# Second feed-forward matmul by Strassen's seven products over pairs of blocks, operands through rings of four slots

## The reference, cut to what matters

```python
x = x + concatenate([y_lru, y_att], axis=-1) @ w_out[i]
h = rmsnorm(x, g_ffn[i])
x = x + square(relu(h @ w_ff1[i])) @ w_ff2[i]
gate = sigmoid(rmsnorm(x, g_ple[i]) @ w_ple_gate[i])
x = x + gate * (p[i] @ w_ple_proj[i])
return rmsnorm(x, g_final)
```

## Time and profile before

| | us |
|---|---|
| median of 3 runs | 1074.56 |
| lowest and highest | 1074.12, 1074.68 |
| span of the profiled execution, first to last instruction | 1072.1 |
| PE busy in it | 1063.0 |
| DVE, ACT, POOL busy | 680.3, 468.1, 416.6 |

### The profile page before, as it was taken

How to read it: one execution, slowest core, us unless ns; L and a number is a source line. 1 busy time by engine, 2 the same in 40 slices (tenths; PEclk the granted TensorE clock), 3 DMA queues, 4 the chain that set the end, 5 groups by cost and what they waited for, 6 DMA issues and landing times.

```text
span 1072.1 us, 13889 instructions
## 1 busy us (share of the span) xinstructions
PE 1063.0 (99%) x4960; PEld 869.5 (81%) x4960; DVE 680.3 (63%) x932; ACT 468.1 (44%) x806; POOL 416.6 (39%) x282
## 2 busy tenths in 40 slices
PE   9999999999999999999999999999999999999997
PEld 7877787777887888888888888888888888888897
DVE  7988787888799643644544544544544544697648
ACT  7467836555683332332332322322322422566334
POOL 0000061334136626516426425435435445295221
PEclk9999999999999999999999999999999999999999
DMA  8111110111011121121111111112112112420004
GB/s 335 40 40 40 40 58 32 40 41 40 0 40 40 40 79 39 39 78 39 39 70 48 39 49 69 39 39 78 39 39 78 39 39 76 159 79 1 1 2 158
DMA packets 20179, 61.06 MB, mean 57 GB/s; under 512 B 2096, under 2 KB 4144, under 8 KB 20144
## 3 DMA queue, kind: packets, MB, share of 16 engines
q1 hardware_dynamic: 19312, 59.56, 15.3%
q10 hardware_dynamic: 832, 1.05, 0.3%
HBM read 56.40 MB, written 4.19 MB: 57 GB/s over the span
## 4 chain that ended last, share of the span: by engine, by line
PE 89%; DVE 6%; ACT 3%; issue 1%; DMA 1%; SPq 0%; POOL 0%; DVEq 0%; ACTq 0%; POOLq 0%
PE bank L611 29%; PE bank L612 28%; PE bank L613 28%; PE bank L726 1%; PE bank L697 1%; ACT raw L1191 1%; DMA stage<-in_w_in 1%; DVE xT L1849 1%; DVE t_lo L1798 1%; PE bank L741 0%; PE bank L756 0%; DVE raw L1792 0%; ACT h_hi L1183 0%; DVE r_ffn L1433 0%; DVE r_mix L1433 0%
## 5 line engine op out<-in xcount | busy, mean ns | idle before, releaser
L611 PE MATMUL bank<-h_hi,w_hi 128*128 128x512 f32 (+1 forms) x722 | 278.5, 386 | 0.6 <-DVE w_lo L1428 0.5
L612 PE MATMUL bank<-h_lo,w_hi 128*128 128x512 f32 (+1 forms) x722 | 274.6, 380 | 0.0
L613 PE MATMUL bank<-h_hi,w_lo 128*128 128x512 f32 (+1 forms) x722 | 274.5, 380 | 0.0
L1849 DVE TENSOR_TENSOR xT<-bank,xT 128x512 f32<-128x512 f32 x256 | 172.3, 688 | 109.8 <-PE bank L613 109.8
L611 PE MATMUL bank<-u_hi,w_hi 128*128 128x512 f32 x512 | 199.8, 390 | 0.2
L613 PE MATMUL bank<-u_hi,w_lo 128*128 128x512 f32 x512 | 199.2, 389 | 0.0
L612 PE MATMUL bank<-u_lo,w_hi 128*128 128x512 f32 x512 | 199.2, 389 | 0.0
L611 PEld LDWEIGHTS bank<-h_hi,w_hi 128*128 128x128 f32 x722 | 135.7, 188 | 35.1 <-issue 6.6
L613 PEld LDWEIGHTS bank<-h_hi,w_lo 128*128 128x128 f32 x722 | 135.8, 188 | 26.1
L612 PEld LDWEIGHTS bank<-h_lo,w_hi 128*128 128x128 f32 x722 | 135.8, 188 | 25.4 <-issue 0.5
L557 POOL TENSOR_TENSOR w_lo<-w_raw,w_hi 128x1024 fp32r<-128x1024 f32 x30 | 73.9, 2485 | 125.6 <-ACT w_hi L1283 117.8
(11 more groups left out here) (238 smaller groups left out, 1727.9 us busy)
## 6 DMA issues: line engine op xcount, KB each, us to landing
w_raw<-in_w_ff SPq DMA_DIRECT2D x60, 512.0 KB, 3.8
stage<-in_w_in SPq DMA_DIRECT2D x13, 512.0 KB, 6.6
stage<-in_w_out SPq DMA_DIRECT2D x8, 512.0 KB, 4.5
stage<-in_w_ple_gate SPq DMA_DIRECT2D x8, 512.0 KB, 3.2
xT<-in_x SPq DMA_DIRECT2D x6, 512.0 KB, 10.9
stage<-in_w_ff SPq DMA_DIRECT2D x4, 512.0 KB, 3.2
out_x<-xT SPq DMA_DIRECT2D x4, 512.0 KB, 3.1
out_x<-xT SPq DMA_DIRECT2D x6, 256.0 KB, 2.2
```

What stands on the lines that cost most here:

```text
L611: pe.matmul(o, whi, hh, start=first, stop=False, skip_group_check=onto)
L612: pe.matmul(o, whi, hl, start=False, stop=False, skip_group_check=onto)
L613: return pe.matmul(o, wlo, hh, start=False, stop=last, skip_group_check=onto)
L1849: dve.tensor_tensor(dst, bank[4 + q % 4][:, :], dst, ALU.add).then_inc(y_added, 1)
```

## The change

Blocks 0 and 1 stay as they were. Blocks 2 to 15 are taken in seven pairs g = 1 to 7. A pair is 28 steps of 12 matmuls. Steps 0 to 13 are the seven first-matmul products of each of its two blocks (s = 0, 1), as before. Steps 14 to 27 are seven Strassen products of the second matmul: product p = 0 to 6 is summed over the pair's two blocks (s = 0, then s = 1), 4 tiles of output each. Products 1, 3 and 5 are added onto the banks of the product before, and DVE reads each of the seven sums into four tiles of xT (`read_sums`). The four quarters of x are not kept as such but in another basis of sums, put in place in front of the first pair (8 operations) and taken out again in the last (`fold`, 8 operations).

The left operand of each step (a weight quarter or a sum of quarters) goes through a ring of four slots: ACT copies the high part (`left_head`) once the step four before is over (`step_over`), POOL subtracts the low part (`left_low`). The right operands of steps 14 to 27 go through a second ring of four (`right_head` on ACT, `right_low` on DVE), and their sums are made by DVE (`right_sum`). POOL makes the weight sums: four for each first block (`w1_front`, `w1_back`) and eight for the pair's second weights (`w2_sum`). The first weights now come in halves, those of the second block of a pair behind `left_low` 3 and 6. The order of the k tiles in `gate` and `ple_high` is changed (FF_ORDER: 4 to 7, then 0 to 3), `pw_lo` moves from DVE to POOL, and the gate's second piece is loaded when steps 26 and 27 are over.

```diff
+PAIRS = FF_BLOCKS // 2
+STEPS = 4 * PRODUCTS
+LEFTS = 4
+RIGHTS = 4
...
+        def step_over(eng, g, t):
...
+            before, t = (1, t + STEPS) if t < 0 else (0, t)
+            if t < 2 * PRODUCTS:
+                eng.wait_ge(prod_done, 2 * PRODUCTS * g + (t - 6 - 2 * PRODUCTS * before))
+            elif t % 2 == 0:
+                eng.wait_ge(sub_done, PRODUCTS * g + ((t - 2 * PRODUCTS) // 2 - 6 - PRODUCTS * before))
+            else:
+                eng.wait_ge(ff2_done, STEPS * g + (4 * ((t - 2 * PRODUCTS) // 2) + 8 - STEPS * before))
...
-            with sp.Fori(2, FF_BLOCKS) as b:
-                sp.wait_ge(prod_done, PRODUCTS * b - PRODUCTS)
-                load_w1(b)
-                load_w2(b)
...
+            with sp.Fori(2, PAIRS) as g:
+                sp.wait_ge(left_ready, counted(10 - STEPS, g))
+                load_w1_half(g, 0, 0)
+                sp.wait_ge(left_ready, counted(17 - STEPS, g))
+                load_w1_half(g, 0, 1)
+                sp.wait_ge(left_ready, counted(27 - STEPS, g))
+                load_w2_pair(g)
+                sp.wait_ge(left_ready, counted(3, g))
+                load_w1_half(g, 1, 0)
+                sp.wait_ge(left_ready, counted(6, g))
+                load_w1_half(g, 1, 1)
...
+            def left_low(g, t):
+                pool.wait_ge(left_high, counted(t, g))
+                pool.tensor_tensor(left_lo[t % LEFTS], left_raw(t), left_hi[t % LEFTS], ALU.subtract
+                                   ).then_inc(left_ready, 1)
...
+            def w1_front(g, s):
...
+                for h in range(2):
+                    pool.wait_ge(w1_half_in[h], 32 * g + 16 * (s - 1))
+                pool.tensor_tensor(a21, a21, a22, ALU.add).then_inc(sum1_made, 1)
+                pool.wait_ge(sum1_made, counted(4 * s, g, 8))
...
+                pool.tensor_tensor(s2_raw(s), a21, a11, ALU.subtract).then_inc(sum1_made, 1)
...
+                pool.wait_ge(sum1_made, counted(4 * s + 1, g, 8))
+                pool.wait_ge(left_ready, counted(PRODUCTS * s + 2, g))
+                pool.tensor_tensor(a21, a22, s2_raw(s), ALU.subtract).then_inc(sum1_made, 1)
+                pool.wait_ge(sum1_made, counted(4 * s + 2, g, 8))
+                pool.tensor_tensor(s2_raw(s), a12, s2_raw(s), ALU.subtract).then_inc(sum1_made, 1)
...
+                    pool.wait_ge(left_ready, counted(2 * PRODUCTS - 1, g))
+                    pool.wait_ge(sum2_made, counted(2 + s, g, 8))
+                    ins = pool.tensor_tensor(s4_raw(s), a21, a12, ALU.subtract)
...
+            def left_pair(g):
+                for s in range(2):
+                    w1_front(g, s)
+                    for i in range(3):
+                        left_low(g, PRODUCTS * s + i)
+                    w1_back(g, s)
+                    for i in range(3, PRODUCTS):
+                        left_low(g, PRODUCTS * s + i)
+                        if s == 1 and i in (3, 4):
+                            w2_sum(g, 0, i - 3)
+                for s in range(2):
+                    left_low(g, 14 + s)
+                    w2_sum(g, 1, s)
+                for s in range(2):
+                    w2_sum(g, 2, s)
+                for t in range(16, 20):
+                    left_low(g, t)
+                for s in range(2):
+                    left_low(g, 20 + s)
+                    w2_sum(g, 3, s)
+                for t in range(22, STEPS):
+                    left_low(g, t)
...
+                pool.wait_ge(pw_high, h + 1)
+                pool.tensor_tensor(pw_lo[:, o], pw_raw[:, o], pw_hi[:, o], ALU.subtract).then_inc(pw_ready, 1)
+            pool.wait_ge(right_ready, counted(2 * PRODUCTS - 1, PAIRS - 1, 2 * PRODUCTS))
...
-            with pe.Fori(2, FF_BLOCKS) as b:
-                for i in range(PRODUCTS):
...
-                    product(b, i)
-                pe.wait_ge(w2_split, 2 * b)
-                ff2(b)
...
+            def second_product(g, p):
+                onto = p in (1, 3, 5)
+                for s in range(2):
+                    t, j = 2 * PRODUCTS + 2 * p + s, 2 * p + s
+                    pe.wait_ge(left_ready, counted(t, g))
+                    pe.wait_ge(right_ready, counted(j, g, 2 * PRODUCTS))
...
+                    for m in range(LT):
+                        if s == 0:
+                            pe.wait_ge(y_added, read_count(g, p - 1, m))
...
+                        if s == 1:
+                            last.then_inc(ff2_done, 1)
+                    if s == 0:
+                        last.then_inc(sub_done, 1)
+            with pe.Fori(1, PAIRS) as g:
+                for t in range(2 * PRODUCTS):
+                    first_product(g, t)
+                for p in range(PRODUCTS):
+                    second_product(g, p)
...
+            def left_head(g, t):
+                step_over(act, g, t - LEFTS)
+                left_raw_in(act, g, t)
+                act.activation(left_hi[t % LEFTS], left_raw(t), ACT.Copy).then_inc(left_high, 1)
+            def right_head(g, j):
+                if j >= RIGHTS:
+                    step_over(act, g, 2 * PRODUCTS + j - RIGHTS)
+                right_raw_in(act, g, j)
+                act.activation(right_hi[:, j % RIGHTS, :], right_raw(j), ACT.Copy).then_inc(right_high, 1)
...
+            def ff_pair(g, last=False):
+                for t in range(LEFTS):
+                    left_head(g, t)
+                for s in range(2):
+                    t = PRODUCTS * s + LEFTS
+                    first_bank(g, s)
+                    for i in range(4):
+                        left_head(g, t + i)
+                        if s == 1 and i == 0:
+                            right_head(g, 0)
+                    hidden_square(g, s, 0)
+                    left_head(g, t + 4)
+                    hidden_square(g, s, 1)
+                    last_bank(g, s)
+                    if s == 1:
+                        right_head(g, 1)
+                        right_head(g, 2)
+                    left_head(g, t + 5)
+                    hidden_square(g, s, 2)
+                    left_head(g, t + 6)
+                    hidden_square(g, s, 3)
+                right_head(g, 3)
+                for j in range(4, 2 * PRODUCTS):
+                    right_head(g, j)
+                    left_head(g, 14 + j)
+                    if last and j < 10:
+                        embedding_high(j - 4)
...
+            def post(g, s):
...
+                product_over(dve, g, PRODUCTS * s + 1)
...
+                dve.tensor_tensor(u2[:, :], bank[1][:, :], u2[:, :], ALU.add).then_inc(u2_made, 1)
+                product_over(dve, g, PRODUCTS * s + 2)
...
+                dve.tensor_tensor(c22, bank[3][:, :], u2[:, :], ALU.add).then_inc(p5_read, 1)
+                product_over(dve, g, PRODUCTS * s + 3)
...
+                dve.tensor_tensor(c22, bank[2][:, :], c22, ALU.add).then_inc(c22_made, 1)
...
+                relu_scale(c22, 0)
+                product_over(dve, g, PRODUCTS * s + 4)
+                dve.tensor_tensor(c12, bank[3][:, :], u2[:, :], ALU.add).then_inc(c12_made, 1)
...
+                relu_scale(c12, 0)
+                if s == 1:
+                    right_sum(g, 0, 1)
...
+                relu_scale(c11, 1)
+                if s == 1:
+                    right_low(g, 1)
+                    right_low(g, 2)
+                product_over(dve, g, PRODUCTS * s + 6)
+                dve.tensor_tensor(c21, bank[2][:, :], u2[:, :], ALU.add).then_inc(c21_made, 1)
...
+                relu_scale(c21, 1)
...
+            def read_sums(g, p):
+                for m in range(LT):
+                    dve.wait_ge(ff2_done, STEPS * g + (4 * p + m + 5))
...
+                    ins.then_inc(y_added, 1)
...
+            def fold(hf, m):
...
+                    ins = dve.tensor_tensor(dst, c22, dst, ALU.add)
...
+                ins.then_inc(folded, 1)
...
+            def hidden_pair(g, last=False):
+                post(g, 0)
+                right_sum(g, 0, 0)
+                right_low(g, 0)
+                post(g, 1)
+                right_low(g, 3)
+                right_sum(g, 1, 0)
+                right_sum(g, 1, 1)
+                for p in range(PRODUCTS):
+                    read_sums(g, p)
+                    if last and p == 4:
+                        for m in range(LT):
+                            fold(0, m)
+                    if last and p == 5:
+                        for m in range(LT):
+                            fold(1, m)
+                            ple_low(m, 0)
+                    if p < 5:
+                        right_low(g, 2 * p + 4)
+                        right_low(g, 2 * p + 5)
+                    if p in (0, 1):
+                        right_sum(g, 2 + p, 0)
+                        right_sum(g, 2 + p, 1)
+                    if last and p in (2, 3):
+                        embedding_low(2 * p - 4)
+                        embedding_low(2 * p - 3)
...
```

(42 more changed lines are left out.)

269 lines of the change are left out of this document (208 added, 61 removed).

## The result

The changed kernel takes 1125.74 us (median of 4 runs, 1123.36 to 1126.25) against 1074.59 us: 1.0475 times as long, with an interval of 1.046 to 1.0489. The forecast was 1084 and its range ended at 1100: the sign was right, the size was not. The profiled execution took 1125.94 us, its span is 1124.1 us.

A forecast was written before the change was run, and what follows sets the result against it. PE, busy 99%, was taken to bound the kernel. From 1072.1 us, less 38.1 saved, plus 7 × 5.1 of stall and 11.5 behind the loop, came 1081.2; with 2.5 for the median, 1084 (range 1056 to 1100).

The forecast's parts named there:

- the saving: Feed-forward loop: 336 matmuls a pair instead of 360, 5.44 us a pair, 38.1 us over seven pairs.
- the stall: In front of step 16 of each pair: PE waits 5.1 us for DVE's read of the first product.
- the path up to it: Within a pair: half load at 13.9, POOL's row to w2_sum(2, 1) at 43.6, ACT's right_head(3) at 45.4 us.
- The step that failed first: DVE ahead of read_sums(g, 0): right_low(3) waits for POOL until 46.1, then three operations at 0.60 end at 47.9 us.
- after the stall there are 1.3 us of slack at step 18 and more later: Rest of the pair behind step 16: PE has 1.3 us in hand at step 18, more later.
- it falls in the stall: Rival, chance 0.14: behind each stall a step runs at half speed, up to 2.72 us a time; 1088 to 1102 us.
- Behind the last pair: After the loop: POOL, tied up until left_low(27), starts pw_lo and the additions late; 11.5 us more (9 to 14).
- a wait that the forecast had seen but placed at `gate(1)`: End of the feed-forward part: after POOL's copy, ACT's square and keep(5), gate(1) can start at +28.3 us.
- The sum: Whole kernel: profiled span 1072.1, less 38.1, plus seven stalls of 5.1, plus 11.5, gives 1081.2 us.

The follow-up runs named there:

- The shortened row: Changed kernel with POOL's low parts of steps 10 to 13 taken over only 16 of each 128 columns: 1109.62 us, 1.0334.
- The measurement of the two engines by themselves: No layer, only rows of 128x512 operations on DVE and POOL: six DVE operations take 3.70 us alone, 9.96 us beside POOL.
- DVE's order: Changed kernel with both right_sum(1) behind read_sums(0) and the later sums one product further back: 1092.34 us, 1.0165.
- The matmuls in the wait: Changed kernel with 24 more matmuls on PE, results unused, between steps 15 and 16 of each pair: 1112.7 us, 1.0356.
- the long wait in the kernel before: Kernel before the change, with PE waiting ahead of ff2 in blocks 2 to 15 for all four low parts of the squared hidden units: 1171.73 us, 1.0914.
- two of POOL's sums early: Changed kernel with reads first, right_head(3) early, both w2_sum(g, 0, s) ahead of POOL's half-load wait, folds behind product 5's reads: 1093.28 us, 1.018.

## Why the prediction was right or wrong

**Right:** the saving (168 matmuls, 38.1 us); the place of the stall, step 16; the path up to it. The half load reached POOL at +13.8 from the pair's start (forecast 13.9), `w2_sum(2, 1)` was done at +42.6 (43.6), `right_head(3)` at +44.3 (45.4). The shortened row confirms that POOL's late sums are a part of it.

**The step that failed first** is the one behind these, "right_low(3), right_sum(1, 0) and right_sum(1, 1) at 0.60: 47.9". It took the earlier trace rows for the rule, a row of DVE operations that holds POOL off, over the earlier trace rows, where the operation took 1.17. The three took 1.70 each: `right_low(3)` ended at +46.0, the sums at +49.3, and the reads let PE go on at +50.0. From `right_head(3)` to there it took 5.7 us in place of 3.2; that the stall came out only 1.4 us longer (6.5 against 5.1) is luck, as the path up to it was 1.1 us shorter than forecast. The measurement of the two engines by themselves shows the turns, DVE's order shows the price: 3.4 us of the wait are the two sums. A DVE operation met by a busy POOL costs DVE 1.70, so what lies ahead of a waiting PE has to be priced at that, not at 0.60 plus one wait.

**The sentence "after the stall there are 1.3 us of slack at step 18 and more later"** failed by the same price. Two `right_low` and two `right_sum` at up to 1.73 stand ahead of `read_sums(2)`, and PE waits 2.2 us at step 20.

**The term that the sum put at nothing** is the clock. As a rival (it falls in the stall) it had 0.14 and up to 2.72 us a time; as part of the forecast it had no term, since the earlier trace rows alone spoke for it. It came true with 2.4 us a pair on the mean. The matmuls in the wait and the long wait in the kernel before show it from both sides. The rival's own range (1088 to 1102) still ended too low, as it kept the stall at 5.1 us and had no second wait. The Trainium skill's warning (TensorE: Matmul & The Clock Gate, HAM oscillation — how this bites in real kernels), that waits between stretches of matmuls can bring the low clock back each time, agrees with the long wait: 4.3 us brought the low clock in all of the 14 blocks, 1.25 us in none. But long waits aren't needed for it. With two of POOL's sums early no wait in the loop was over 2.4 us, and the clock fell in each of the first six pairs.

**Behind the last pair** the forecast was 11.5 us, and it is 11.7, but that is luck, as the place was wrong. PE waits 5.7 us ahead of step 26, by the starts of its matmuls (8.5 up to its first `project` matmul, with the low clock behind the wait), as the reads of product 5 stand behind four folds of 1.98 us each; from that matmul (997.20) to the end it takes only 3.2 us longer than before (126.9 against 1072.1 − 948.36 = 123.7 us). The forecast had these folds only as a burden on POOL. With the folds out of the way (two of POOL's sums early), 5.6 us of waiting for ACT's `keep` show up in `project`, a wait that the forecast had seen but placed at `gate(1)`.

**The sum** against the span, with what was measured: 1072.1 − 38.1 + 7 × (6.5 + 2.2 + 2.5) + 11.7 = 1124.1. The 2.5 are the low clock and gaps of 0.1 us. Of the 42.9 us that the forecast lacked, 9.8 are the longer stall (7 × 1.4), 15.4 the second wait and 17.5 the clock with these gaps. So the price of DVE's operations accounts for 25 us and the clock for 17: with either of the two put right alone, the forecast would still have been more than 17 us short.

## What to carry to other kernels

Where PE adds onto banks that another engine must read first, that engine's queue is PE's path: put each read ahead of everything that PE doesn't need sooner, and price what stands in front of it as it runs beside the busy neighbour, not as it runs alone. The work saved on PE paid only once the order was right, DVE's above all (1125.7 to 1070.4 us with the same work, two sums of POOL and one copy of ACT moved as well), and even then 3.4 us of 38.1 arrived. Removing the shortest of three waits gave 0.2 us a pair, while the others brought the low clock. A wait of PE has two prices, its length and the low clock behind it: 4.3 us of it in each block cost 7. The second price can't be read from one pair: look at several, as the same waits bring the low clock in some and not in others.

## What the runs showed of the hardware

- Two-SBUF-input operations on DVE and POOL's, 128x512 in float32, take turns, whoever is first, in rows of six and of ten: DVE's go from 0.60 to some 1.70 us, POOL's from 1.22 to some 1.70. The row of four in the earlier trace rows did not, and that is unexplained. The Trainium skill (SBUF — State Buffer, Who interferes with whom) has one of them blocked for the whole of the other's instruction. The trace agrees nearly: from start to start a turn takes 1.67 us (DVE and POOL by themselves), 0.15 less than 0.60 and 1.22 together.
- With one DVE operand in PSUM nothing of this happens: ten in 6.07 us, POOL's four in 4.94.
- PE's granted clock falls to 0.50 behind idling, but the length of a wait doesn't tell it. A single wait of 1.25 us in 42 us, or of 1.6 us in 78.6, never brought the low clock there; one of 4.3 us in 48 brought it each time and cost 2.7 us. In between it is unsteady: waits of 3.1 and 2.2 us a pair brought it in three of six pairs (1.6 to 3.0 us), waits of 0.9, 1.3 and 2.3 us in two of six or in four of six, waits of 1.25 and 2.35 us in all six (1.6 us). What decides between them no run here shows.
